# PEER gates marked and gated in one VectorE operation per token, and the last gate tile stored in four portions beside the experts

## The chip, the cores and the metric

The kernel runs on one core of a Trainium2 chip. The metric is the device time of one execution in microseconds (us); lower is better. A core has five engines that run their own instruction streams and meet through semaphores: TensorE (PE, matmuls), VectorE (DVE), ScalarE (ACT), GpSimd (POOL) and SyncE (SP, which here only starts transfers). Sixteen DMA engines move data between HBM (the memory outside) and SBUF (the memory inside, 128 partitions). PSUM is where matmuls leave their results.

## What is computed

The program is a two-part network. Its first part has two layers, each with a mixer and a PEER feed-forward block (a block with 128 x 128 = 16384 tiny experts, of which every token picks 128). Only PEER matters here:

```
def peer_ffn(h, w_query, sub_keys, expert_u, expert_v):
    ...
    idx = jnp.take_along_axis(cand_i, pos, axis=-1).reshape(t_count, PEER_HEADS * PEER_TOPK)
    gate = jax.nn.softmax(top_s, axis=-1).reshape(t_count, PEER_HEADS * PEER_TOPK).astype(h.dtype)
    def block(args):
        tb, ib, gb = args
        act = jax.nn.gelu(jnp.einsum('pkd,pd->pk', expert_u[ib], tb), approximate=False) * gb
        return jnp.einsum('pk,pkd->pd', act, expert_v[ib])
```

A chosen expert's number is first key x 128 + second key. Layer 0 works on 512 tokens, layer 1 on 256.

## The kernel before

**No gather.** The kernel computes all 16384 experts for all tokens, 128 at a time (one first key, called a row here), and multiplies by a gate that is zero where a token did not pick the expert. So it needs the gates spread out: for each first key i, a table [second key, token].

**`peer_scatter`** makes that table. `selT` holds, on 128 partitions (a token's 128 picks), the first key, the second key and the gate of each token. For one token the product of a [pick, second key] matrix B (one-hot of the second key times the gate) and a [pick, first key] matrix A (one-hot of the first key) is its 128 x 128 table of gates. The work goes in sets of 8 tokens with two buffers (x = 0, 1). In one set

- VectorE compares key numbers (bf16) with the second keys (L1752), with the first keys (L1754), and multiplies the second marks by the gates into fp32 `second_ind` (L1758), each for 8 tokens at once, 1024 elements wide;
- ScalarE widens the first marks to fp32 `first_ind` (L1784) and copies two PSUM banks of four tokens each into the stage (L1788);
- TensorE does eight matmuls (L1773; a profile shows each as two records of 128x128).

Sixteen sets are one tile of 128 tokens; layer 0 has four tiles (64 sets), layer 1 two (32 sets), 96 sets in all. A finished tile of 8 MB (64 KB in each partition) is stored by SP to the HBM tensor `gates` [first key, second key, token] (L1816) in pieces of 512 B, out of two stages in turn. Only the last store of a layer has nothing of `peer_scatter` beside it: SP waits for it (L1818) before the block ends. After its last tile ScalarE and VectorE also split the normed activations into two terms (`TwoTerms`, L1841 to L1851).

**`experts_wide`** (layer 0) and **`experts_narrow`** (layer 1) then run over the 128 rows. SP loads row i's weights `u_stream` and `v_stream` (512 KB each) and its gates `g_stream` (256 KB wide, 128 KB narrow: contiguous 2 KB or 1 KB in each partition). ScalarE and VectorE split u into two parts (L1967 and L2015 wide, L2172 and L2212 narrow), TensorE forms dots (L1929, L2133), ScalarE applies Gelu, VectorE the gate (L2026, L2218), both split that too and v (L1973, L2020; L2184, L2223), and TensorE multiplies with v (L1942, L2143). Wide, the dots of row groups of four are formed ahead; narrow, of two rows ahead. Nothing of these loads starts before `peer_scatter` has ended. Buffers of the experts lie in SBUF where the stages were.

Order on each engine is the order written; a `Fori` is a loop on the chip.

Of the kernel before, what the change touches and what calls it, by code (L numbers as in the profile page):

```python
# [48 lines left out]
class Signal:  # L49
# [9 lines left out]
    def done(self, n):  # L59
        self.base += n  # L60
# [474 lines left out]
class AdaParams:  # L535
# [9 lines left out]
    def __init__(self, k, ctx, layer, ada_w, params, consts, mod, fetch=True, first=0, groups=6 * D // BANK):  # L545
# [5 lines left out]
        self.slot = [k.sig(f"ada_slot{n}") for n in range(self.TURN)]  # L551
# [1153 lines left out]
def peer_scatter(k, selT, T, consts, gates, even, terms):  # L1705
# [8 lines left out]
    GROUP = 2 * SET  # L1714
    TURNS = P // GROUP
    ALL = tiles * TURNS
    first, widened, second, gated, joined, taken = (
        k.sig("sc_" + x) for x in ("first", "widened", "second", "gated", "joined", "taken"))
    ready = k.sig("sc_keys")
    written = [k.sig("sc_written0"), k.sig("sc_written1")]  # L1720
    with ExitStack() as ctx:
        stage = (even, k.sb(ctx, "gate_stage_odd", [P, P]))
        numbers = k.sb(ctx, "key_numbers", [P, 2], BF16)
        keys = k.sb(ctx, "keys_16", [2, T], BF16)
        is_first = k.sb(ctx, "is_first", [2, SET // 2, P, 2], BF16)
        is_second = k.sb(ctx, "is_second", [2, SET // 2, P, 2], BF16)
# [4 lines left out]
        number4 = numbers[:].rearrange("p (q n) a -> p q n a", q=1).broadcast_to([P, SET // 2, P, 2])  # L1731

        def here(i, x):
            return bass.ds(i * GROUP + SET * x, SET)

        def by_token(marks):
            return marks.rearrange("p q n a -> p q a n")

        with nc.Block() as block:
            @block.vector  # L1740
            def _(dve):
                dve.sem_inc(gated.h, 2)
                dve.tensor_copy(numbers[:], C("iota").rearrange("p (n a) -> p n a", a=1).broadcast_to([P, P, 2]))
                dve.tensor_copy(keys[:], selT[:, 0:2, :]).then_inc(ready.h, 1)
                dve.wait_ge(ready.h, ready.at(1))
                with dve.Fori(0, ALL) as i:
                    for x in range(2):
                        def marks(row):
                            return keys[:, row, here(i, x)].rearrange("p (q n a) -> p q n a", n=1, a=2).broadcast_to([P, SET // 2, P, 2])

                        dve.wait_ge(gated.h, gated.at(1 + x) + i * 2)
                        dve.tensor_tensor(is_second[:, x], number4, marks(1), ALU.is_equal).then_inc(second.h, 1)  # L1752
                        dve.wait_ge(widened.h, widened.at(1 + x) + i * 2)
                        dve.tensor_tensor(is_first[:, x], number4, marks(0), ALU.is_equal).then_inc(first.h, 1)  # L1754
                        dve.wait_ge(second.h, second.at(1 + x) + i * 2)
                        dve.wait_ge(joined.h, joined.at(2 * x + 2) + i * 4)
                        gate = selT[:, 2, here(i, x)].rearrange("p (q a n) -> p q a n", n=1, a=2).broadcast_to([P, SET // 2, 2, P])
                        dve.tensor_tensor(B[:, x].rearrange("p (q a) n -> p q a n", a=2), by_token(is_second[:, x]), gate, ALU.mult).then_inc(gated.h, 1)  # L1758
                terms.vector(dve)

            @block.tensor
            def _(pe):
                pe.sem_inc(joined.h, 4)
                with pe.Fori(0, ALL) as i:
                    for b in range(4):
                        x = b // 2
                        if b % 2 == 0:
                            pe.wait_ge(widened.h, widened.at(3 + x) + i * 2)
                            pe.wait_ge(gated.h, gated.at(3 + x) + i * 2)
                        pe.wait_ge(taken.h, taken.at(1 + b) + i * 4)  # L1770
                        for a in range(4):
                            n = 4 * (b % 2) + a
                            m = pe.matmul(ps[:, b, a * P:a * P + P], B[:, x, n], A[:, x, n], start=True, stop=True)  # L1773
                        m.then_inc(joined.h, 1)

            @block.scalar
            def _(act):
                act.sem_inc(taken.h, 4)
                act.sem_inc(widened.h, 2)

                def widen(i, x):
                    act.wait_ge(first.h, first.at(1 + x) + i * 2)
                    act.wait_ge(joined.h, joined.at(2 * x + 2) + i * 4)
                    act.activation(A[:, x].rearrange("p (q a) n -> p q a n", a=2), by_token(is_first[:, x]), ACT.Copy).then_inc(widened.h, 1)  # L1784

                def take(i, tile, at, b):
                    act.wait_ge(joined.h, joined.at(5 + b) + i * 4)
                    act.activation(stage[tile % 2][:, :, bass.ds(at + 4 * b, 4)], ps[:, b, :].rearrange("p (t n) -> p n t", t=4), ACT.Copy).then_inc(taken.h, 1)  # L1788

                for tile in range(tiles):  # L1790
                    t0 = tile * TURNS
                    widen(t0, 0)
                    widen(t0, 1)
                    if tile >= 2:
                        act.wait_ge(written[tile % 2].h, written[tile % 2].at(DMA_DONE * (tile // 2)))
                    take(t0, tile, 0, 0)
                    take(t0, tile, 0, 1)
                    with act.Fori(0, TURNS - 1) as n:
                        i = n + t0
                        at = n * GROUP  # L1800
                        widen(i + 1, 0)
                        take(i, tile, at, 2)
                        take(i, tile, at, 3)
                        widen(i + 1, 1)
                        take(i + 1, tile, at + GROUP, 0)
                        take(i + 1, tile, at + GROUP, 1)
                    take(t0 + TURNS - 1, tile, P - GROUP, 2)
                    take(t0 + TURNS - 1, tile, P - GROUP, 3)
                act.wait_ge(written[0].h, written[0].at(DMA_DONE * (tiles // 2)))
                terms.scalar(act)  # L1810

            @block.sync
            def _(sp):
                for tile in range(tiles):
                    sp.wait_ge(taken.h, taken.at(4 + (tile + 1) * TURNS * 4))
                    sp.dma_start(gates[:, :, tile * P:tile * P + P].rearrange("i p t -> p i t"), stage[tile % 2][:]).then_inc(written[tile % 2].h, DMA_DONE)  # L1816
                for w in written:
                    sp.wait_ge(w.h, w.at(DMA_DONE * tiles // 2))  # L1818
    terms.done()
    ready.done(1)  # L1820
    for x in (first, second):
        x.done(2 * ALL)
    for x in (gated, widened):
        x.done(2 * ALL + 2)
    for x in (joined, taken):
        x.done(4 * ALL + 4)
    for w in written:
        w.done(DMA_DONE * tiles // 2)
# [29 lines left out]
def experts_wide(k, u, v, gates, h, acc, xT, gain, us):  # L1858
# [10 lines left out]
    with ExitStack() as ctx:  # L1869
        ub = k.sb(ctx, "u_stream", [4, DC, P])  # L1870
        vb = k.sb(ctx, "v_stream", [2, D])
        vs = k.sb(ctx, "v_parts", [4, 2, D], F32R)
        gb = k.sb(ctx, "g_stream", [4, T])
        act = k.sb(ctx, "acts", [2, T])
# [3 lines left out]
        with nc.Block() as block:  # L1878
            @block.sync
            def _(sp):  # L1880
# [5 lines left out]
                def get_g(s, j, first):  # L1886
                    if not first:
                        sp.wait_ge(gated.h, s * 4 + gated.at(j - 3))
                    sp.dma_start(gb[:, j], gates[bass.ds(s * 4 + j, 1)].rearrange("a p t -> (a p) t")).then_inc(g_in[j].h, DMA_DONE)
# [72 lines left out]
            def _(sc):  # L1962
# [120 lines left out]
def experts_narrow(k, u, v, gates, h, xT, gain, us, spare, ident):  # L2083
# [12 lines left out]
    with ExitStack() as ctx:  # L2096
        ub = k.sb(ctx, "u_stream", [RAW, DC, P])
        vb = k.sb(ctx, "v_stream", [RAW, D])
        vs = k.sb(ctx, "v_parts", [RING, 2, D], F32R)
        act = k.sb(ctx, "acts", [RING, T])  # L2100
        aparts, gb = spare
        sums = vb[:, 0:2]
        pd = k.banks(ctx, 4, "pd")
        po = k.banks(ctx, 4, "po")
        with nc.Block() as block:
            @block.sync
            def _(sp):
                def get(n, j, first):
                    if not first:
                        sp.wait_ge(u_split.h, n + u_split.at(j + 1 - RAW))  # L2110
                    sp.dma_start(ub[:, j], u[bass.ds(n + j, 1)].rearrange("a p c e -> p (a c) e")).then_inc(u_in[j].h, DMA_DONE)
                    if not first:
                        sp.wait_ge(gated.h, n + gated.at(j + 1 - RAW))
                    sp.dma_start(gb[:, j], gates[bass.ds(n + j, 1)].rearrange("a p t -> (a p) t")).then_inc(g_in[j].h, DMA_DONE)
                    if not first:
# [1166 lines left out]
```

## Time and profile before

| what | value |
|---|---|
| runs before | 4536.93, 4542.0, 4542.59 us (median 4542.0) |
| span of the profiled execution | 4538.3 us, between the fastest and the median of these runs |
| PE, DVE, ACT busy | 3652.0 (80%), 2230.0 (49%), 1566.0 (35%) us |
| DMA | 909.64 MB in 331813 packets, mean 200 GB/s |
| scatter, layer 0 | from about 996 us to the last tile's store at 1151.54 us |
| scatter, layer 1 | to the last tile's store at 2588.33 us |
| one store of 8192 KB | 30.3 us from issue to landing |

The profile times the instructions of one execution. Its span runs from the first to the last of them; the page gives no other time of that execution, so the span stands beside the runs of the kernel as it is. PE's share is an average over stages with different limits; what counts for this change is what is waited for in the two scatters and just behind them.

### The profile page before, as it was taken

To read this page: it belongs to the slowest core of one execution; us is meant where nothing else is said; L and a number is where in the kernel's file an instruction comes from. 1 tells how busy PE (TensorE), PEld (TensorE's weight loads), DVE (VectorE), ACT (ScalarE), POOL (GpSimd) and SP (SyncE) were. 2 spreads that over 40 slices of the span, in tenths; PEclk is the share of its full clock that TensorE was granted. 3 is DMA by queue.
4 is the path that set the end of the run, shared out by engine and by line. 5 is a ranking of instruction groups with operands and counts; after the bars stand their busy time and mean duration, and the time that the engine had idled before them with its cause. 6 is when DMAs were issued, how large, how long until landed. Compare 5 with 4: busy or idle time off the path is not lost. (4 is left out here: it accounts for less than half of the span.)

```text
span 4538.3 us, 58330 instructions
## 1 busy us (share of the span) xinstructions
PE 3652.0 (80%) x19637; PEld 2640.8 (58%) x19637; DVE 2230.0 (49%) x4378; ACT 1566.0 (35%) x2639; POOL 168.9 (4%) x344
## 2 busy tenths in 40 slices
PE   5977977968699999998796689998368667777776
PEld 3747965447588888886565579997236322222223
DVE  3634643899566666665358778884441100000001
ACT  3433432128444444443241666663121111011111
POOL 0006610000000000000000000000000000000000
PEclk8988988979899999999897899999659788788878
DMA  4230021516644454443201499994212499999996
GB/s 161 73 132 13 13 96 52 210 45 199 217 175 182 185 185 175 168 173 126 98 20 65 126 362 312 312 312 140 116 38 84 189 428 427 427 427 428 427 428 273
DMA packets 331813, 909.64 MB, mean 200 GB/s; under 512 B 46592, under 2 KB 167168, under 8 KB 306176
## 3 DMA queue, kind: packets, MB, share of 16 engines
q1 hardware_dynamic: 331648, 907.42, 52.9%
q8 instruction: 106, 1.74, 0.2%
q14 instruction: 59, 0.48, 0.0%
HBM read 854.38 MB, written 52.95 MB: 200 GB/s over the span
## 5 line engine op out<-in xcount | busy, mean ns | idle before, releaser
L1929 PE MATMUL pd<-h_parts,u_parts 128*128 128x512 f32 x2048 | 471.3, 390 | 37.5 <-DVE u_parts L2015 37.5
L1942 PE MATMUL po<-act_parts,v_parts 128*128 128x512 f32 x2048 | 483.6, 393 | 10.3 <-DVE v_parts L2020 3.7
L1929 PEld LDWEIGHTS pd<-h_parts,u_parts 128*128 128x128 f32 x2048 | 385.6, 188 | 118.1 <-DVE u_parts L2015 37.7
L1942 PEld LDWEIGHTS po<-act_parts,v_parts 128*128 128x128 f32 x2048 | 383.6, 189 | 105.4 <-DVE v_parts L2020 22.4
L3053 PE MATMUL pb<-moe_ring,moe_xs 128*32 128x512 f32 x2048 | 334.4, 759 | 137.1 <-DMA moe_ring<-in_moe_gu 119.3
L3104 DVE TENSOR_TENSOR moe_hidden<-moe_silu,pg 128x512 f32<-128x512 f32 x16 | 11.0, 688 | 659.6 <-PE pg L3042 533.1
L2133 PE MATMUL pd<-h_parts,u_parts 128*128 128x256 f32 x2048 | 268.2, 284 | 38.6 <-DVE u_parts L2212 38.6
L2133 PEld LDWEIGHTS pd<-h_parts,u_parts 128*128 128x128 f32 x2048 | 264.6, 192 | 50.3 <-DVE u_parts L2212 39.2
L2143 PE MATMUL po<-v_parts,act_parts 128*128 128x512 f32 x1024 | 260.0, 398 | 0.9 <-DVE act_parts L2228 0.9
L395 PE MATMUL ps<-h_terms,w_terms 128*128 128x512 f32 x960 | 225.1, 398 | 40.6 <-DVE w_terms L408 40.6
L3069 PE MATMUL pd<-moe_ring,moe_hidden 128*32 128x512 f32 x1024 | 167.4, 790 | 100.6 <-DMA moe_ring<-in_moe_down 87.9
L1979 ACT ACTIVATE acts<-pd 128x512 f32<-128x512 f32 x128 | 76.7, 599 | 486.0 <-PE pd L1929 486.0
L395 PEld LDWEIGHTS ps<-h_terms,w_terms 128*128 128x128 f32 x960 | 184.8, 193 | 81.5 <-DVE w_terms L408 42.5
L3089 ACT ACTIVATE moe_part<-pb 128x512 f32<-128x512 f32 x128 | 76.3, 597 | 451.4 <-PE pb L3053 451.3
L3053 PEld LDWEIGHTS pb<-moe_ring,moe_xs 128*32 128x32 f32 x2048 | 67.0, 124 | 280.7 <-DMA moe_ring<-in_moe_gu 142.6
L1773 PE MATMUL ps<-first_ind,second_ind 128*128 128x128 f32 x1536 | 198.2, 284 | 38.9 <-ACT first_ind L1784 28.9
L3042 PEld LDWEIGHTS pg<-consts,moe_part 128*128 128x128 f32 x1024 | 140.5, 215 | 130.9 <-issue 129.6
L1773 PEld LDWEIGHTS ps<-first_ind,second_ind 128*128 128x128 f32 x1536 | 182.2, 195 | 55.3 <-issue 54.9
L2143 PEld LDWEIGHTS po<-v_parts,act_parts 128*128 128x128 f32 x1024 | 185.3, 190 | 35.2 <-DVE v_parts L2223 1.1
L2040 DVE TENSOR_TENSOR hT<-hT,po 128x512 f32<-128x512 f32 x248 | 159.1, 682 | 90.1 <-PE po L1942 90.0
L1538 PE MATMUL pq<-hT,w_stream 128*128 128x512 f32 (+1 forms) x512 | 173.3, 498 | 27.0 <-PEq L568 15.0
L2223 DVE SCALAR_TENSOR_TENSOR v_parts<-v_stream,v_parts 128x1024 fp32r<-128x1024 f32 x128 | 156.8, 1225 | 63.4 <-ACT v_parts L2184 63.4
(472 smaller groups left out, 5846.8 us busy)
## 6 DMA issues: line engine op xcount, KB each, us to landing
moe_ring<-in_moe_gu SPq DMA_DIRECT2D x128, 2048.0 KB, 26.3
u_stream<-in_peer_u SPq DMA_DIRECT2D x256, 512.0 KB, 6.0
v_stream<-in_peer_v SPq DMA_DIRECT2D x256, 512.0 KB, 4.3
moe_ring<-in_moe_down SPq DMA_DIRECT2D x64, 2048.0 KB, 26.2
ada_ring<-in_ada_w SPq DMA_DIRECT2D x24, 2048.0 KB, 13.4
g_stream<-peer_gates SPq DMA_DIRECT2D x128, 256.0 KB, 5.9
peer_gates<-gate_stage_even SPq DMA_DIRECT2D x3, 8192.0 KB, 30.3
peer_gates<-gate_stage_odd SPq DMA_DIRECT2D x3, 8192.0 KB, 30.3
```

The lines of the kernel that those rows point to most:

```text
L395: m = pe.matmul(ps[:, ch % BANKS, 0:T], ws[:, r, w, c], parts[:, x, c], start=(c + w + x == 0), stop=(c == kc - 1 and w == 1))
L1538: m = pe.matmul(pq[:, ch % 2, 0:T], stream.wb[:, g % 2, c, (ch % 4) * P:(ch % 4) * P + P], hT[:, c, 0:T], start=(c == 0), stop=(c == DC - 1))
L1773: m = pe.matmul(ps[:, b, a * P:a * P + P], B[:, x, n], A[:, x, n], start=True, stop=True)
L1929: m = pe.matmul(pd[:, j, 0:T], us[:, j, w, c], h[:, w, c], start=(c + w == 0), stop=(c == DC - 1 and w == 1))
L1942: m = pe.matmul(po[:, (c + b) % 4, 0:T], vs[:, j, w, (c + b) * P:(c + b) * P + P], aparts[:, 4 * half + j, w], start=(j + w == 0), stop=(j ...
L2040: dve.tensor_tensor(acc[:, c], acc[:, c], po[:, c % 4, 0:T], ALU.add).then_inc(added.h, 1)
L2133: m = pe.matmul(pd[:, j % RING, 0:T], us[:, j % RING, w, c], h[:, w, c], start=(c + w == 0), stop=(c == DC - 1 and w == 1))
L2143: m = pe.matmul(po[:, 2 * t + half], aparts[:, r, w, t * P:t * P + P], vs[:, r, w, half * BANK:half * BANK + BANK], start=(start and w == ...
L2223: dve.scalar_tensor_tensor(out=vs[:, j % RING, 1], in0=vb[:, j], scalar=FAR / STEP, in1=vs[:, j % RING, 0].bitcast(F32), op0=ALU.mult, op1 ...
L3042: m = pe.matmul(pg[:, n // 4, a * CAP:a * CAP + CAP], part[:, n % 2, j * P:j * P + P], stacked, start=True, stop=True)
L3053: m = pe.matmul(pb[32 * q:32 * q + 32, n % 2, :], xs[:, u % 2, c], w[:, c, :], start=(c < 4), stop=(c >= 4))
L3069: m = pe.matmul(pd[32 * j:32 * j + 32, b, :], hid[:, a * CAP:a * CAP + CAP], w[:, j, b * BANK:(b + 1) * BANK], start=(g == 0), stop=(g == ...
```

## The change

It has four parts.

1. **VectorE in a set.** The comparison of second keys and the multiplication with gates for 8 tokens become eight `tensor_scalar` operations, one a token: fp32 key numbers 0 to 127 compared with a [128, 1] operand (the second key of each partition) and multiplied with another (the gate). Bf16 first marks are made for 6 of 8 tokens only and widened by ScalarE as before, now 768 elements; for the other two tokens VectorE writes `first_ind` itself with a `tensor_scalar` that has one [128, 1] operand. The loops are written out.
2. **Layout of `gates`.** Now [tile, second key, first key, token in tile]: a stage goes out as 64 KB contiguous in each partition, and a row's gates come in as pieces of 512 B, one per partition and tile.
3. **The last tile.** ScalarE starts its store itself in four portions (first keys 0 to 31, 32 to 63, ...), each with its own semaphore, ahead of its share of `TwoTerms`, and the block does not wait for them. The experts wait portion by portion where they read gates or overwrite the stage.
4. **Places in SBUF** of the experts' buffers are ordered for that, and the narrow ones are halved.

```
-                with dve.Fori(0, ALL) as i:
-                    for x in range(2):
-                        ...
-                        dve.tensor_tensor(is_second[:, x], number4, marks(1), ALU.is_equal).then_inc(second.h, 1)
-                        dve.tensor_tensor(is_first[:, x], number4, marks(0), ALU.is_equal).then_inc(first.h, 1)
-                        dve.tensor_tensor(B[:, x].rearrange("p (q a) n -> p q a n", a=2), by_token(is_second[:, x]), gate, ALU.mult).then_inc(gated.h, 1)
+                for n in range(ALL):
+                    x, t0 = n % 2, n * SET
+                    marks = keys[:, t0:t0 + WIDE].rearrange("p (q n a) -> p q n a", n=1, a=2).broadcast_to([P, PAIRS, P, 2])
+                    if n >= 2:
+                        dve.wait_ge(widened.h, widened.at(n - 1))
+                    dve.tensor_tensor(is_first[:, x], number4, marks, ALU.is_equal).then_inc(first.h, 1)
+                    if n >= 2:
+                        dve.wait_ge(joined.h, joined.at(2 * n - 2))
+                    for j in range(SET):
+                        if j >= WIDE:
+                            dve.tensor_scalar(A[:, x, j], iota, key(0, t0 + j), None, ALU.is_equal)
+                        m = dve.tensor_scalar(B[:, x, j], iota, key(1, t0 + j), key(2, t0 + j), ALU.is_equal, ALU.mult)
+                        if j % 4 == 3:
+                            m.then_inc(gated.h, 1)
...
+                act.wait_ge(taken.h, taken.at(2 * ALL))
+                last.write(act, gates, stage[(tiles - 1) % 2])
                 act.wait_ge(written[0].h, written[0].at(DMA_DONE * (tiles // 2)))
                 terms.scalar(act)
...
-                    sp.dma_start(gates[:, :, tile * P:tile * P + P].rearrange("i p t -> p i t"), stage[tile % 2][:]).then_inc(written[tile % 2].h, DMA_DONE)
+                    sp.dma_start(gates[tile], stage[tile % 2][:]).then_inc(written[tile % 2].h, DMA_DONE)
...
+    def write(self, eng, gates, stage):
+        for n in range(self.PARTS):
+            rows = slice(n * self.ROWS, (n + 1) * self.ROWS)
+            eng.dma_start(gates[self.tile, :, rows], stage[:, rows]).then_inc(self.landed[n].h, DMA_DONE)
...
 # experts_wide, SP
                 for j in range(4):
+                    get_u(1, j, False)
+                last.wait(sp, 0)
+                for j in range(4):
                     get_g(0, j, True)
-                for j in range(4):
-                    get_u(1, j, False)
                 period(0, True)
+                last.wait(sp, 1, 2, 3)
...
 # experts_wide, ScalarE
                     high_u(1, j)
+                    if j == 0:
+                        last.wait(sc, 1, 2, 3)
                     high_a(0, 0, j, True)
...
 # experts_narrow, SP
+                for j in range(HALF):
+                    get_u(0, j)
+                last.wait(sp, 0)
+                for j in range(HALF):
+                    get_g(0, j)
+                    get_v(0, j)
+                for j in range(HALF, RAW):
+                    get_g(0, j)
+                last.wait(sp, 1, 2)
+                for j in range(HALF, RAW):
+                    get_u(0, j)
+                last.wait(sp, 3)
+                for j in range(HALF, RAW):
+                    get_v(0, j)
```

HALF is 4 and RAW 8. In `experts_narrow` ScalarE waits for portion 1 before it splits v of row 2.

VectorE, at the beginning of the scatter of layer 0, before: one turn of the loop, two sets (ISA and REGISTER_ALU rows are waits and their arithmetic).

```order
L1752 TENSOR_TENSOR is_second<-key_numbers,keys_115 128x1024
L1754 ISA
L1754 TENSOR_TENSOR is_first<-key_numbers,keys_115 128x1024
L1756 ISA
L1758 ISA
L1758 TENSOR_TENSOR second_ind<-is_second,sel_T 128x1024
```

And of the change, the same place, one set:

```order
L1747 TENSOR_TENSOR is_first<-key_numbers,keys_116 128x768
L1753 TENSOR_SCALAR second_ind<-consts,sel_T 128x128 x6
L1752 TENSOR_SCALAR first_ind<-consts,sel_T 128x128
L1753 TENSOR_SCALAR second_ind<-consts,sel_T 128x128
L1752 TENSOR_SCALAR first_ind<-consts,sel_T 128x128
L1753 TENSOR_SCALAR second_ind<-consts,sel_T 128x128
```

Three operations of a set have become eleven, ten of them 128 elements wide.

SyncE, at the end of the scatter of layer 0 and the start of `experts_wide`, before:

```order
L1816 DMA peer_gates<-gate_stage_even 128x128x128
L1816 DMA peer_gates<-gate_stage_odd 128x128x128
L1739 UNCONDITIONAL_BRANCH
L1879 UNCONDITIONAL_BRANCH
L1884 DMA u_stream<-in_peer_u 128x1024 x4
L1889 DMA g_stream<-peer_gates 128x512 x4
L1884 DMA u_stream<-in_peer_u 128x1024 x4
```

And of the change:

```order
L1805 DMA peer_gates<-gate_stage_odd 128x16384
L1805 DMA peer_gates<-gate_stage_even 128x16384
L1733 UNCONDITIONAL_BRANCH
L1890 UNCONDITIONAL_BRANCH
L1895 DMA u_stream<-in_peer_u 128x1024 x8
L1900 DMA g_stream<-peer_gates 128x4x128 x4
```

The fourth store has left SP's queue, all eight first u loads stand ahead of the gates, and a gate load is 128 x 4 pieces.

ScalarE, at the end of the scatter of layer 1, of the change:

```order
L1831 DMA peer_gates<-gate_stage_odd 128x4096 x4
L1862 ACTIVATE h_parts<-hT 128x256 x8
L1733 UNCONDITIONAL_BRANCH
L2209 UNCONDITIONAL_BRANCH
L2216 ACTIVATE u_parts<-u_stream 128x1024 x3
L2222 ACT_TABLE_LOAD
```

The four portions stand ahead of the eight ACTIVATEs of `TwoTerms`; before, those followed the last copy directly.

## Rows read from the trace of the kernel before

**Rows 1.** Windows: a scatter tile, wide experts, start and middle of narrow experts.

```profile
1037.00:1075.00 38.00, 32.54 (x259) 29.79 (x257) 37.65 (x49) 32.61 (x49) 0.00 (x0) 1.00 0.76 221
1500.00:1800.00 300.00, 298.67 (x1304) 243.68 (x1303) 198.54 (x243) 126.28 (x163) 0.00 (x0) 1.00 0.48 175
2640.00:2700.00 60.00, 60.00 (x383) 54.46 (x382) 51.56 (x67) 42.46 (x66) 0.00 (x0) 1.00 1.04 397
2900.00:3000.00 100.00, 100.00 (x635) 90.57 (x634) 82.39 (x106) 68.18 (x106) 0.00 (x0) 1.00 0.90 309
```

Columns: stretch, length, busy us (and instructions) of PE, PEld, DVE, ACT, POOL, granted TensorE clock, DMA share, GB/s.

**Rows 2.** Timeline of one scatter set of layer 0 (start us, us, instruction, count).

```profile
1141.45 0.68 DVE L1752 TENSOR_TENSOR is_second<-key_numbers,keys 128x1024 bf16<-128x1024 bf16 x1
1141.49 1.06 ACT L1788 ACTIVATE gate_stage_odd<-ps 128x512 f32 x2
...
1141.77 2.05 PE L1773 MATMUL ps<-first_ind,second_ind 128*128 128x128 f32 x16 [0.29 <-ACT first_ind L1784]
1142.06 0.68 DVE L1754 TENSOR_TENSOR is_first<-key_numbers,keys 128x1024 bf16<-128x1024 bf16 x1
1142.66 1.22 DVE L1758 TENSOR_TENSOR second_ind<-is_second,sel_T 128x1024 f32<-128x1024 bf16 x1
1142.85 1.06 ACT L1784 ACTIVATE first_ind<-is_first 128x1024 f32<-128x1024 bf16 x1 [0.30 <-DVE is_first L1754]
1143.80 0.68 DVE L1752 TENSOR_TENSOR is_second<-key_numbers,keys 128x1024 bf16<-128x1024 bf16 x1
```

**Rows 3.** Groups by line and shape, VectorE (busy us, mean ns; idle before).

```profile
L1758 DVE TENSOR_TENSOR second_ind<-is_second,sel_T 128x1024 f32<-128x1024 bf16 x96 | 116.7, 1215 | 2.6 <-PE ps L1773 2.6
L2419 DVE TENSOR_SCALAR att_s<-att_s,att_stats 128x512 f32<-128x512 f32 x32 | 15.6, 486 | 1.1
L2419 DVE TENSOR_SCALAR att_s<-att_s,att_stats 128x256 f32<-128x256 f32 x24 | 8.5, 353 | 0.9
L1841 DVE TENSOR_SCALAR hT<-hT 128x256 f32<-128x256 f32 x8 | 1.7, 280 | 0.0
```

**Rows 4.** Timeline, two trains of eight VectorE operations.

```profile
2382.37 3.26 DVE L526 SCALAR_TENSOR_TENSOR hT<-xT,mod_mult,rstd 128x256 f32<-128x256 f32 x8
2585.31 1.69 DVE L1841 TENSOR_SCALAR hT<-hT 128x256 f32<-128x256 f32 x8
```

**Rows 5.** Timeline from the last store of layer 0 to the first dots.

```profile
1151.41 4.26 ACT L1851 ACTIVATE h_parts<-hT 128x512 fp32r<-128x512 f32 x8
1151.54 0.37 SPq L1816 DMA_DIRECT2D peer_gates<-gate_stage_odd  x1
1152.06 4.90 DVE L1845 SCALAR_TENSOR_TENSOR h_parts<-h_parts,hT 128x512 fp32r<-128x512 f32 x8 [0.74 <-ACT h_parts L1851]
1182.35 1.77 SPq L1884 DMA_DIRECT2D u_stream<-in_peer_u  x4
...
1185.97 1.06 ACT L1967 ACTIVATE u_parts<-u_stream 128x1024 fp32r<-128x1024 f32 x1 [30.31 <-DMA u_stream<-in_peer_u]
...
1188.34 26.82 PE L1929 MATMUL pd<-h_parts,u_parts 128*128 128x512 f32 x110 [37.47 <-DVE u_parts L2015]
```

**Rows 6.** The same in layer 1, and the dots of row 4.

```profile
2588.20 2.55 ACT L1851 ACTIVATE h_parts<-hT 128x256 fp32r<-128x256 f32 x8
2588.33 0.38 SPq L1816 DMA_DIRECT2D peer_gates<-gate_stage_odd  x1
2588.64 2.77 DVE L1845 SCALAR_TENSOR_TENSOR h_parts<-h_parts,hT 128x256 fp32r<-128x256 f32 x8 [1.55 <-ACT h_parts L1851]
2619.13 0.35 SPq L2111 DMA_DIRECT2D u_stream<-in_peer_u  x1
...
2625.22 3.74 PE L2133 MATMUL pd<-h_parts,u_parts 128*128 128x256 f32 x16 [37.55 <-DVE u_parts L2212]
...
2640.93 2.08 PE L2133 MATMUL pd<-h_parts,u_parts 128*128 128x256 f32 x16
```

**Rows 7.** DMA in 4100 to 4400 us, where packets of 16 KB are loaded.

```profile
DMA packets 8800, 128.26 MB, mean 428 GB/s; under 512 B 972, under 2 KB 972, under 8 KB 972
```

More of the change, by code:

```diff
@@ L1713, in peer_scatter @@
     SET = 8
[L1714 to L1718, printed above, removed]
+    PAIRS = 3
+    WIDE = 2 * PAIRS
+    PER = P // SET
+    ALL = tiles * PER
+    first, widened, gated, joined, taken = (k.sig("sc_" + x) for x in ("first", "widened", "gated", "joined", "taken"))
     ready = k.sig("sc_keys")
@@ L1729, in peer_scatter @@
         ps = k.banks(ctx, 4)
[L1731 to L1737, printed above, removed]
+        number4 = numbers[:].rearrange("p (q n) a -> p q n a", q=1).broadcast_to([P, PAIRS, P, 2])
+        iota = C("iota")
         with nc.Block() as block:
@@ L1790, in _, with widen @@
[L1790 to L1794, printed above, removed]
-                        act.wait_ge(written[tile % 2].h, written[tile % 2].at(DMA_DONE * (tile // 2)))
[L1796 to L1808, printed above, removed]
+                def widen(n):
+                    act.wait_ge(first.h, first.at(n + 1))
+                    if n >= 2:
+                        act.wait_ge(joined.h, joined.at(2 * n - 2))
+                    act.activation(A[:, n % 2, 0:WIDE].rearrange("p (q a) n -> p q a n", a=2),
+                                   is_first[:, n % 2].rearrange("p q n a -> p q a n"), ACT.Copy).then_inc(widened.h, 1)
@@ new lines, in take @@
+                def take(n, b):
+                    tile, at = n // PER, (n % PER) * SET + 4 * b
+                    act.wait_ge(joined.h, joined.at(2 * n + b + 1))
+                    act.activation(stage[tile % 2][:, :, at:at + 4], ps[:, 2 * (n % 2) + b, :].rearrange("p (t n) -> p n t", t=4), ACT.Copy).then_inc(taken.h, 1)
+                widen(0)
+                widen(1)
+                for n in range(ALL):
+                    tile = n // PER
+                    if n % PER == 0 and tile >= 2:
+                        act.wait_ge(written[tile % 2].h, written[tile % 2].at(DMA_DONE * (tile // 2)))
+                    take(n, 0)
+                    take(n, 1)
+                    if n + 2 < ALL:
+                        widen(n + 2)
@@ L1855, in done, with experts_wide @@
         self.high.done(DC)
-def experts_wide(k, u, v, gates, h, acc, xT, gain, us):
+def experts_wide(k, u, v, gates, h, acc, xT, gain, us, last):
     nc = k.nc
@@ L2080, in experts_wide, with experts_narrow @@
     added.done(N_SUPER * DC)
-def experts_narrow(k, u, v, gates, h, xT, gain, us, spare, ident):
+def experts_narrow(k, u, v, gates, h, xT, gain, us, spare, ident, last):
     nc = k.nc
@@ L2107, in _ @@
             def _(sp):
[L2108 to L2115, printed above, removed]
-                        sp.wait_ge(v_split.h, n + v_split.at(j + 1 - RAW))
-                    sp.dma_start(vb[:, j], v[bass.ds(n + j, 1)].rearrange("a p d -> (a p) d")).then_inc(v_in[j].h, DMA_DONE)
@@ L2188, in high_a, with step @@
                     sc.activation(aparts[:, j % RING, 0], act[:, j % RING], ACT.Copy, scale=1.0 / FAR).then_inc(a_high.h, 1)
-                def step(n, j, start=False, last=False):
+                def step(n, j, start=False, end=False):
                     early = start and j < RING
-                    if not (last and j >= TURN - 2):
+                    if not (end and j >= TURN - 2):
                         high_u(n, j + 2, start and j + 2 < RING)
                     squash(n, j, early)
+                    if start and j == 2:
+                        last.wait(sc, 1)
                     high_v(n, j, early)
```

158 lines of the change are left out of this document (88 added, 70 removed).

## The prediction

> **What bounds the kernel now.** I read the windows first. In a scatter tile VectorE is busy 37.65 of 38.00 us, TensorE 32.54 and ScalarE 32.61; the clock is full and the DMA engines have room [rows 1]. The timeline of one set then shows who waits: VectorE's operations touch each other and the set repeats after 1143.80 - 1141.45 = 2.35 us, while ScalarE waits 0.30 us for VectorE's first marks and TensorE 0.29 us for ScalarE [rows 2]. So VectorE's three steps, 0.61 + 0.60 + 1.14 us from start to start, are the scatter, in 96 sets [rows 2, 3]. Behind it comes a hole: the last store is issued at 1151.54, the first u load at 1182.35 and the first dots are formed at 1188.34; in layer 1 it is 2588.33, 2619.13 and 2625.22 [rows 5, 6]. TensorE stands still for 37.5 us each time, 30.8 of it the store. Behind that TensorE is full (298.67 of 300 us wide, 100 of 100 narrow), with DMA at 0.48 and 0.90 of its time [rows 1]. The change touches both places, VectorE's work and the hole, and loads gates in smaller pieces where TensorE is full.
>
> **Part 1: a set on VectorE.** What counts is the time from start to start. No row shows a 128-element `tensor_scalar` with [128, 1] operands in a train, so I build it up. Without such an operand, 256 wide: (1.69 - 0.28)/7 = 0.201 us [rows 3, 4]. From 512 to 256 elements the same operation loses 486 - 353 = 133 ns, so 128 fewer are worth 67 ns, and a 128-wide one takes 0.134 us; of that 0.067 us is fixed [rows 3]. A [128, 1] operand: eight 256-wide operations with one take 3.26 us, eight without 2.77 us, that is 0.061 us each [rows 4, 6]; the durations 353 and 280 ns say 0.073 [rows 3]. So 0.195 us with one operand. The bf16 comparison shrinks to 768 elements: (0.61 - 0.07) x 0.75 + 0.07 = 0.475 us. A set is then 0.475 + 10 x 0.195 = 2.425 us if a second operand costs nothing more, against 2.34: +0.085 x 96 = **+8 us**. This is the term that decides, and its bounds are wide:
>
> - Below, the operand costs nothing in such a train: 0.475 + 10 x 0.134 = 1.82 us. Then others bound the set. ScalarE needs 2.35 - 0.30 = 2.05 us now, and its widening loses 256 elements at (4.26 - 2.55)/8 = 0.214 us per 256 [rows 5, 6]: 1.83. TensorE's 16 records take 2.05 us with the tail, about 1.9 in a train [rows 2]. With hand-overs some 1.95 us: -0.39 x 96 = -37 us.
> - Above, the second operand costs another 0.061 us: 0.475 + 8 x 0.256 + 2 x 0.195 = 2.91 us, +0.57 x 96 = +55 us.
>
> I take the middle, since both rows with one operand show its price and none shows it hidden, and two operands side by side may well be fetched in one go. The Trainium skill speaks to both sides. "VectorE: DVE Perf Modes" (section on the TRN2 errata) gives 58 + elements/2 cycles at 0.96 GHz for such an operation, operands or not, 0.127 us; by it a set would be 1.75 us on VectorE, which is the lower bound's case; the 0.061 us in this trace is not in that formula. "ScalarE: Activation LUTs" (what ACT_TABLE_LOAD costs) says that on ScalarE each [128, 1] operand adds its own time; carried over to VectorE that would be the upper bound's case. No row here shows two.
>
> The ends of the scatter get shorter. Now, after VectorE's last 1.22 us operation eight matmuls and a copy follow; then only four do, and the first matmul of a layer waits for four small operations instead of two comparisons and a wide product. I estimate 2 us a layer, **-4 us**. Written-out loops cost only fetching of instructions; nothing shows a wait for that now, zero.
>
> **Parts 2 and 3: the store.** It moves 8.39 MB. With 512 B pieces it takes 30.3 us (277 GB/s). With pieces of 16 KB the load stretch reaches 428 GB/s [rows 7], which would be 19.6 us; no row shows such a store, so its bounds are 19.6 and 30.3; I take 20, as the piece size is that of the 428 row.
>
> *Layer 0.* Count from the last copy. ScalarE issues four portions, as SP's four u loads do in 1.77 us [rows 5]; so `TwoTerms`, hidden until now, ends not 5.4 but 7.2 us after it (1152.06 + 4.90 = 1156.96 before). This is the price of losing its cover. SP issues u at 7.7; the first dots could be formed 6.0 us later, at 14. But the store shares the DMA engines. Before the dots of row 4 can be formed, store, five u rows (2.6 MB) and four gate rows (1.05 MB) are to be moved, 12.1 MB, 28 us at 428 GB/s: at 30 + 2.4 for the split = 32. Before, they were formed at 36.8 + 2 for the low clock + 4 x 3.68 = 53.5 (a row's dots are half of 300/1304 x 32 = 7.36 us [rows 1]). Gain 21. ScalarE's wait for portions 1 to 3 behind row 0 holds the split of u for row 5 and every gate product behind it; with the store landed by 25 it costs little, I take 18. With a store at 277 GB/s the same sum gives 38.9 + 2 + 2.4, gain 10.
>
> *Layer 1.* Before u of row 4 is there: the store, u and v of four rows (4.2 MB), eight gate rows (1.05) and u (0.5), 14.2 MB, 33 us, so dots of row 4 at 37 against 2640.93 - 2588.33 = 52.6 [rows 6]: gain 15. With the slow store 47, gain 6. Together **-33 us**, bounds -16 and -48 (dots at 14 and 11.5 us instead of 36.8 and 36.9, if nothing of the store stood in the way).
>
> *Gate loads in 512 B pieces.* Narrow, a row needs 1.18 MB in 3.78 us. When pressed, the DMA engines moved 397 GB/s [rows 1], 2.97 us a row. If 128 KB of gates go at the old store's 277 GB/s they need 0.47 us, at 428 0.31: at most 0.2 more. Room is 0.8 us, cost nothing. Wide has twice the room. If that cover were gone, each 0.1 us over 3.78 would cost 13 us.
>
> **Sum.** +8 - 4 - 33 = -29 us against the profile's span of 4538.3, which lies 3.7 under the median; against the median 4542 this gives 4513.
>
> **Rivals.**
>
> - *The operand is hidden*: a set of 1.95 us, -37 instead of +8: 4538 - 37 - 4 - 33, against the median 4468. For it: the eight operations depend on nothing near. Against: the 0.061 us in a train of independent ones.
> - *The second operand costs as much as the first*: +55 - 4 - 33 = +18, 4560. It is slower from 2.73 us a set on, that is from 0.04 us for the second operand. This is the one on the other side. For it: nothing shows two at once. Against: nothing either.
> - *The store stands in the way of the experts' first loads.* Four portions are queued first and may be served first; then the hole is filled hardly at all and the gain of 33 shrinks to some 10: +8 - 4 - 10, 4536. For it: no row shows a store beside loads. Against: the pressed windows show three kinds of loads from one queue sharing 397 GB/s [rows 1], and pieces of 16 KB leave more of that than pieces of 512 B.
> - *Gathered gates are slow.* Pieces of one partition pair lie 64 KB apart. Above 1.3 us for 128 KB (under 100 GB/s) narrow rows wait for DMA; at 80 GB/s 1.64 us, +0.3 x 128 = +40: 4553. "DMA: Bandwidth & Descriptors" (Latency and other measured facts) in the Trainium skill reports copies that slow to 207 GB/s and less where rows lie 512 KB and more apart. The old store wrote pieces 256 KB apart and reached 277 GB/s.
>
> **How the numbers follow.** Forecast 0.45 (4513, its own range 4500 to 4528), operand hidden 0.27, second operand paid 0.14, store in the way 0.09, slow gathers 0.05. The range 4462 to 4545 holds the first, second and fourth, 0.81. A measurement of this kernel tells about 0.2%, 9 us, from no change. Faster by more: 0.45 + 0.27 + 0.04 (half of the fourth) = 0.76 and a little; same: 0.06; slower: 0.17, the second operand and most of the slow gathers.
>
> **What would show it.** The scatter tile's length in the windows: 38.8 us if right, 31 if the operand is free, 46 if paid twice. A 128-wide `tensor_scalar` with two operands should last 0.28 us and repeat after 0.195. TensorE's idle before the first dots should fall from 37.5 us to some 16 in both layers, followed by short waits in rows 1 to 5. Portions should land in about 5 us each. Narrow rows must keep 3.78 us; if they don't, the gathers are slow. I am wrong above all if the pitch of the two-operand operation is not near 0.195 us.

## The result and the profile after

The changed kernel is slower: 4568.09 us (median of 4 runs, 4566.57 to 4572.35) against 4541.89 for the kernel before (4 runs beside it, 4536.93 to 4542.59), ratio 1.0062, 95% interval 1.0048 to 1.0075. The forecast of 4513 has the wrong sign, and its range ended at 4545. The profiled execution took 4566.57 us with a span of 4564.7, 26.4 more than the span of 4538.3 before.

Windows of the changed kernel: a scatter tile, narrow experts, and the second network from the update of x at the end of layer 1 to the first matmuls of its own experts (columns as in [rows 1]).

```profile
1040.00:1085.00 45.00, 35.25 (x248) 29.81 (x248) 45.00 (x172) 28.49 (x48) 0.00 (x0) 1.00 0.44 187
2700.00:3000.00 300.00, 300.00 (x1920) 273.36 (x1920) 249.58 (x321) 206.44 (x321) 0.00 (x0) 1.00 0.94 322
3137.60:3603.50 465.90, 292.04 (x1118) 209.21 (x1122) 161.42 (x409) 85.08 (x221) 0.73 (x2) 0.72 0.21 78
```

VectorE is now busy 45.00 of 45.00 us, and TensorE and ScalarE for a smaller share than before. The timeline of one set (start us, us, instruction; in brackets how long the engine stood idle before it, and what ended that):

```profile
1080.24 0.55 DVE L1747 TENSOR_TENSOR is_first<-key_numbers,keys 128x768 bf16<-128x768 bf16 x1
...
1080.71 1.62 DVE L1753 TENSOR_SCALAR second_ind<-consts,sel_T 128x128 f32<-128x128 f32 x6
1080.83 0.84 ACT L1778 ACTIVATE first_ind<-is_first 128x768 f32<-128x768 bf16 x1 [1.09 <-DVE is_first L1747]
...
1081.92 1.13 PE L1769 MATMUL ps<-first_ind,second_ind 128*128 128x128 f32 x8 [0.38 <-ACT first_ind L1778]
1082.25 0.28 DVE L1752 TENSOR_SCALAR first_ind<-consts,sel_T 128x128 f32<-128x128 f32 x1
1082.44 0.34 DVE L1753 TENSOR_SCALAR second_ind<-consts,sel_T 128x128 f32<-128x128 f32 x1
1082.70 0.28 DVE L1752 TENSOR_SCALAR first_ind<-consts,sel_T 128x128 f32<-128x128 f32 x1
1082.89 0.34 DVE L1753 TENSOR_SCALAR second_ind<-consts,sel_T 128x128 f32<-128x128 f32 x1
1083.15 0.55 DVE L1747 TENSOR_TENSOR is_first<-key_numbers,keys 128x768 bf16<-128x768 bf16 x1
```

The set repeats after 1083.15 - 1080.24 = 2.91 us, to the hundredth the upper bound of the forecast, against 2.34 of before; a tile of sixteen sets takes 46.6 us. An operation with one operand lasts 0.28 us, with two 0.34. From start to start the comparison takes 0.47, one with one operand 0.19 to 0.20, and one with two (1.62 - 0.34)/5 = 0.256.

The end of layer 0's scatter and the first dots, where [rows 5] stood:

```profile
1183.51 0.60 ACT L1784 ACTIVATE gate_stage_odd<-ps 128x512 f32<-128x512 f32 x1 [0.80 <-PE ps L1769]
1184.14 3.17 ACTq L1831 DMA_DIRECT2D peer_gates<-gate_stage_odd  x4
...
1187.40 4.27 ACT L1862 ACTIVATE h_parts<-hT 128x512 fp32r<-128x512 f32 x8 [3.30 <-issue]
1188.07 4.91 DVE L1856 SCALAR_TENSOR_TENSOR h_parts<-h_parts,hT 128x512 fp32r<-128x512 f32 x8 [3.04 <-ACT h_parts L1862]
1193.23 21.92 SPq L1895 DMA_DIRECT2D u_stream<-in_peer_u  x8
1205.69 1.06 ACT L1980 ACTIVATE u_parts<-u_stream 128x1024 fp32r<-128x1024 f32 x1 [14.02 <-DMA u_stream<-in_peer_u]
...
1208.06 30.87 PE L1942 MATMUL pd<-h_parts,u_parts 128*128 128x512 f32 x128 [24.59 <-DVE u_parts L2030]
```

TensorE's idle time fell from 37.47 to 24.59 us, and its 128 matmuls of dots (eight rows) then run in one piece. In layer 1, where [rows 6] stood:

```profile
2643.92 3.79 PE L2177 MATMUL pd<-h_parts,u_parts 128*128 128x256 f32 x16 [20.90 <-DVE u_parts L2258]
2650.89 5.58 PE L2177 MATMUL pd<-h_parts,u_parts 128*128 128x256 f32 x32 [3.18 <-DVE u_parts L2258]
...
2664.02 2.64 PE L2177 MATMUL pd<-h_parts,u_parts 128*128 128x256 f32 x16 [1.91 <-DVE u_parts L2258]
```

There the dots begin 20.90 us after the scatter's last matmul (37.55 before), but wait 3.18 us behind row 0 and 1.91 before row 4.

From issue to landing (least, median, most), a full store of the changed kernel and then its eight portions:

```profile
DMA to landing us min/median/max: 22.6/22.7/22.9
```

```profile
DMA to landing us min/median/max: 6.3/14.3/23.4
```

**Where the 26.4 us are.** The traces are cut at the same instructions: the start of VectorE's first operation for the scatter, the end of the last copy out of PSUM, the start of the last addition to the layer's output (layer 0) or of the update of x (layer 1), and the first matmul of the second network's experts. Times are in us.

| stage | before | after | difference |
|---|---|---|---|
| scatter, layer 0 | 156.0 | 189.0 | +33.0 |
| last copy to the last addition, layer 0 | 992.4 | 979.4 | -13.0 |
| scatter, layer 1 | 80.0 | 95.7 | +15.7 |
| last copy to the update of x, layer 1 | 528.5 | 513.7 | -14.8 |
| second network up to its experts | 460.0 | 465.9 | +5.9 |

Scatter +48.7, experts -27.8, second network +5.9: +26.8. The changed kernel reaches its first scatter 0.4 us earlier, and the stretches between the layers and behind the table are the same to 0.1 us.

### The profile page after: what moved, and what is told of

Same layout as the page of the kernel before. It is cut to its first block and busy times, and to the rows that moved or that the text cites. A ratio compares the mean times of both kernels' runs of the same rounds, so it can differ in the third digit from the quotient of the medians.

```text
span 4564.7 us, 57706 instructions
## 1 busy us (share of the span) xinstructions
PE 3671.7 (80%) x19637; PEld 2655.1 (58%) x19637; DVE 2286.7 (50%) x5146; ACT 1545.7 (34%) x2639; POOL 168.0 (4%) x344
## 3 DMA queue, kind: packets, MB, share of 16 engines
q8 instruction: 119, 1.95, 0.2%
## 5 line engine op out<-in xcount | busy, mean ns | idle before, releaser
L1955 PE MATMUL po<-act_parts,v_parts 128*128 128x512 f32 x2048 | 483.4, 393 | 10.5 <-DVE v_parts L2035 3.9
L1942 PE MATMUL pd<-h_parts,u_parts 128*128 128x512 f32 x2048 | 471.3, 390 | 24.6 <-DVE u_parts L2030 24.6
L1769 PE MATMUL ps<-first_ind,second_ind 128*128 128x128 f32 x1536 | 222.4, 290 | 63.1 <-ACT first_ind L1778 34.6
L1753 DVE TENSOR_SCALAR second_ind<-consts,sel_T 128x128 f32<-128x128 f32 x768 | 221.9, 343 | 0.0
```

Of the source, the lines that this page charges most:

```text
L1753: m = dve.tensor_scalar(B[:, x, j], iota, key(1, t0 + j), key(2, t0 + j), ALU.is_equal, ALU.mult)
L1769: m = pe.matmul(ps[:, 2 * x + b, a * P:a * P + P], B[:, x, 4 * b + a], A[:, x, 4 * b + a], start=True, stop=True)
L1942: m = pe.matmul(pd[:, j, 0:T], us[:, j, w, c], h[:, w, c], start=(c + w == 0), stop=(c == DC - 1 and w == 1))
L1955: m = pe.matmul(po[:, (c + b) % 4, 0:T], vs[:, j, w, (c + b) * P:(c + b) * P + P], aparts[:, 4 * half + j, w], start=(j + w == 0), stop=(j ...
```

## The experiments

My theory after the result: VectorE sets the scatter, and every [128, 1] operand of a `tensor_scalar` costs 0.06 us for itself, the second as much as the first. A rival is that the second ALU operation of the instruction costs the time; another, that something else holds the sets. The kernel before ran again, 13 times beside the first four kernels (median 4539.58) and 13 times beside the last four (4538.69). Intervals are of 95%; where a row of a stage is named, it is as in the table above.

### The gate's operand left out

```
-  m = dve.tensor_scalar(B[:, x, j], iota, key(1, t0 + j), key(2, t0 + j), ALU.is_equal, ALU.mult)
+  m = dve.tensor_scalar(B[:, x, j], iota, key(1, t0 + j), 1.0, ALU.is_equal, ALU.mult)
```

> The change, but the eight operations of a set multiply with the immediate 1.0 instead of the gate operand: gates are left out, marks alone are spread. Theory 1 (the price hangs on the number of [128, 1] operands): start to start 0.195 instead of 0.255 us, a set of 2.43 us, 46 us less than the change, 4522 us. Rival (the price hangs on the second ALU operation): 0.255 us stays and so does 4568 us.

Measured: 4521.0 us (4517.2 to 4523.91), ratio to before 0.9956, interval 0.9939 to 0.9973. It leaves the gates out; the work of the engines is otherwise the same. The timeline of VectorE:

```profile
1081.21 0.54 DVE L1747 TENSOR_TENSOR is_first<-key_numbers,keys 128x768 bf16<-128x768 bf16 x1
1081.68 1.25 DVE L1753 TENSOR_SCALAR second_ind<-consts,sel_T 128x128 f32<-128x128 f32 x6
...
1083.64 0.55 DVE L1747 TENSOR_TENSOR is_first<-key_numbers,keys 128x768 bf16<-128x768 bf16 x1
```

The set is 2.43 us, and the operation repeats after (1.25 - 0.27)/5 = 0.196 us. The multiplication is still in it, by 1.0, so the 0.06 us hang on the operand and not on the second ALU operation. The set is, to 0.01 us, the one I had forecast for the real kernel.

### Both operands left out

```
-  m = dve.tensor_scalar(B[:, x, j], iota, key(1, t0 + j), key(2, t0 + j), ALU.is_equal, ALU.mult)
+  m = dve.tensor_scalar(B[:, x, j], iota, float(j), 1.0, ALU.is_equal, ALU.mult)
```

> As the run without gates, and the key is an immediate too, so the eight operations have no [128, 1] operand (second keys and gates are left out). Theory 1: start to start 0.134 us; VectorE needs 0.475 + 0.39 + 8 x 0.134 = 1.94 us, close to TensorE's 1.9 and ScalarE's 1.83, a set of about 2.0 us, 87 us less than the change, 4481 us. Rival (a floor for 128-wide operations near 0.19 us whatever their operands): the same as without gates, 4522 us.

Measured: 4473.96 us in one run, span 4472.1. VectorE's timeline:

```profile
1079.46 0.56 DVE L1747 TENSOR_TENSOR is_first<-key_numbers,keys 128x768 bf16<-128x768 bf16 x1
1079.94 0.91 DVE L1753 TENSOR_SCALAR second_ind<-consts 128x128 f32<-128x128 f32 x6
...
1081.41 0.56 DVE L1747 TENSOR_TENSOR is_first<-key_numbers,keys 128x768 bf16<-128x768 bf16 x1
```

(0.91 - 0.23)/5 = 0.136 us, and the set 1.95. The three prices 0.136, 0.196 and 0.256 lie on a line. The sum of VectorE's operations, 0.47 + 8 x 0.136 + 2 x 0.20, is the set, so down to 1.95 us no other engine holds it, and operand by operand the time of the scatter follows.

### All first marks made wide

```
-    PAIRS = 3
+    PAIRS = 4
```

All eight first marks are then made by the bf16 comparison and widened by ScalarE (256 words more are kept free ahead of the odd stage).

> The change, but bf16 marks for all eight first keys, widened by ScalarE; VectorE makes none of them itself. Theory 1: 0.61 + 8 x 0.255 = 2.65 us a set against 2.91, 25 us less, 4543 us. Rival (ScalarE, with 2.05 us of work and its hand-overs, holds the set longer): 2.8 us or more, 4557 us.

Measured: 4541.21 us (10 runs, 4535.97 to 4543.75), ratio 1.0003, interval 0.9993 to 1.0012.

```profile
1079.91 0.69 DVE L1747 TENSOR_TENSOR is_first<-key_numbers,keys 128x1024 bf16<-128x1024 bf16 x1
1080.51 2.14 DVE L1753 TENSOR_SCALAR second_ind<-consts,sel_T 128x128 f32<-128x128 f32 x8
1082.56 0.69 DVE L1747 TENSOR_TENSOR is_first<-key_numbers,keys 128x1024 bf16<-128x1024 bf16 x1
```

The set is 2.65 us. Two operations of 0.196 us for 0.13 us of a wide comparison were a loss of 0.26 us a set, 25 us in 96 sets: of the 49 us that the scatter grew by, about half come from taking two first keys into VectorE. ScalarE had the room for them.

Its second network, with the same code, took 460.9 us against 465.9 of the changed kernel, at a granted clock of 0.74 against 0.72:

```profile
3114.50:3575.50 461.00, 287.25 (x1118) 205.03 (x1122) 161.32 (x409) 85.07 (x221) 0.73 (x2) 0.74 0.21 79
```

### The old marks with the new store

```
+    dve.tensor_tensor(is_second[:, x], number4, marks(1), ALU.is_equal)
     dve.tensor_tensor(is_first[:, x], number4, marks(0), ALU.is_equal)
-    for j in range(SET):
-        ...
+    gate = selT[:, 2, t0:t0 + SET].rearrange(...).broadcast_to([P, PAIRS, 2, P])
+    dve.tensor_tensor(B[:, x].rearrange(...), is_second[:, x].rearrange(...), gate, ALU.mult)
```

Only VectorE's part is undone (PAIRS is 4, 1536 words more are kept free ahead of the odd stage). Stages, portions and loads are those of the change.

> The change, but with VectorE's marks and gates made 8 tokens at a time as in the kernel before (loops written out, all first keys by ScalarE); layout, portions and waits of the change are kept. Theory 1 (the second [128, 1] operand costs another 0.061 us, so a set takes 2.91 us, and that is all that the change lost): sets of 2.34 us, a layer-0 tile of 37.5 us, 0.57 x 96 = 55 us less than the change, 4513 us. Rival (something in the new layout or the portions costs time in the experts): 4530 us or more.

Measured: 4514.43 us (4511.33 to 4521.01), ratio 0.9945, interval 0.9928 to 0.9962. But for kernels that leave work out, it is the fastest here together with the one that issues three portions later (4513.27, below). The scatter takes 154.3 and 79.0 us, 1.7 and 1.0 less than before, and the experts 978.6 and 518.0 against 992.4 and 528.5, -24.3 us. The parts add up: the store's is a gain of 24 to 28 us, VectorE's a loss of 49 to 51. The next four kernels are built on this one, and their timelines are to be held against its own:

```profile
1144.58 0.60 ACT L1787 ACTIVATE gate_stage_odd<-ps 128x512 f32<-128x512 f32 x1 [0.29 <-PE ps L1772]
...
1154.31 20.62 SPq L1898 DMA_DIRECT2D u_stream<-in_peer_u  x7
1166.76 1.06 ACT L1983 ACTIVATE u_parts<-u_stream 128x1024 fp32r<-128x1024 f32 x1 [14.01 <-DMA u_stream<-in_peer_u]
...
1169.13 6.04 PE L1945 MATMUL pd<-h_parts,u_parts 128*128 128x512 f32 x16 [24.59 <-DVE u_parts L2033]
```

Its last copy ends at 1144.58 + 0.60 = 1145.18, and its first dots begin 23.95 us later (20.3 in layer 1).

### All portions waited for before the block ends

```
                 for tile in range(max(0, tiles - 3), tiles - 1):
                     sp.wait_ge(written[tile % 2].h, written[tile % 2].at(DMA_DONE * (tile // 2 + 1)))
+                last.wait(sp, 0, 1, 2, 3)
```

> The kernel with the old VectorE method in the new structure (4514 us), with one wait added: SyncE waits for all four portions before the scatter block ends, so nothing of the experts starts beside the store. Theory 1 (starting the experts beside the store gained 13 us in layer 0 and 15 in layer 1 in the change's trace, against a 30.3 us store): the portions need some 20 us, so the block ends about 20 + 3 us behind the last copy and dots 6 us later, at 30 instead of 24 and 20 us: 4514 + 6 + 10 = 4530 us; the layout (pieces of 64 KB) and not the overlap gave the rest. Rival (the overlap gave all of it): 4542 us.

Measured: 4519.79 us (4515.16 to 4521.43), ratio 0.9957, interval 0.9941 to 0.9974.

```profile
1145.85 3.17 ACTq L1835 DMA_DIRECT2D peer_gates<-gate_stage_odd  x4
...
1167.44 7.81 SPq L1899 DMA_DIRECT2D u_stream<-in_peer_u  x5
...
1174.94 1.65 PE L1946 MATMUL pd<-h_parts,u_parts 128*128 128x512 f32 x3 [29.75 <-DVE u_parts L2034]
```

No load runs beside the store, and still all but 5.4 us of the gain are there (6.3 in the two stretches of experts). With four runs of each, from 4511 to 4521 us, so small a difference is hardly clear of noise. My expectation was too high by 10. The store is over 21.6 us after its first portion's issue, 9 earlier than one with 512 B pieces [rows 5], so the larger pieces (16 KB in a portion) are the bigger half. In layer 1 the dots begin 7.6 us later than with the overlap (27.8 against 20.3 us from the last copy), and x is updated at the same distance (518.1 against 518.0): there the overlap gives nothing that this trace shows, though kernels with the same expert code differ by 4 us in that stretch.

### Portions 1 to 3 behind the split of the activations

ScalarE issues only portion 0 at the end of the scatter, and the other three at the start of the experts:

```
-                last.write(act, gates, stage[(tiles - 1) % 2])
+                last.write(act, gates, stage[(tiles - 1) % 2], (0,))
...
 # experts_wide and experts_narrow, ScalarE
+                last.write(sc, gates, odd, (1, 2, 3))
```

> The kernel with the old VectorE method in the new structure (4514 us), but only portion 0 is issued ahead of TwoTerms; portions 1 to 3 are issued by ScalarE as its first step in the experts, beside SyncE's first u loads. Theory 1 (the first u load took 12.5 us instead of 3.6 because 8 MB were queued ahead of it): first dots some 6 us earlier in both layers, but the portions land 8 us later and ScalarE and SyncE wait for them in rows 1 to 4, so the sum is within 5 us of 4514. Rival (a load is slow beside any store, however late that one is queued): the first dots stay at 24 and 20 us behind the last copy and 4520 us.

Measured: 4513.27 us (4510.34 to 4519.58), ratio 0.9947, interval 0.9931 to 0.9964.

```profile
1145.63 0.60 ACT L1787 ACTIVATE gate_stage_odd<-ps 128x512 f32<-128x512 f32 x1 [0.30 <-PE ps L1772]
...
1152.59 1.90 ACTq L1834 DMA_DIRECT2D peer_gates<-gate_stage_odd  x3
1162.63 1.06 ACT L1983 ACTIVATE u_parts<-u_stream 128x1024 fp32r<-128x1024 f32 x1 [11.62 <-DMA u_stream<-in_peer_u]
...
1165.00 10.37 PE L1945 MATMUL pd<-h_parts,u_parts 128*128 128x512 f32 x32 [19.41 <-DVE u_parts L2034]
1168.72 1.06 ACT L1983 ACTIVATE u_parts<-u_stream 128x1024 fp32r<-128x1024 f32 x1 [5.03 <-DMA u_stream<-in_peer_u]
...
1174.85 1.06 ACT L1983 ACTIVATE u_parts<-u_stream 128x1024 fp32r<-128x1024 f32 x1 [5.08 <-DMA u_stream<-in_peer_u]
```

The last copy ends at 1146.23, so the dots begin 18.8 us behind it in layer 0, and 14.3 in layer 1: 5.2 and 5.9 us earlier than in the kernel it is built on, as expected. In layer 0 that is still 5 us behind the 14 that the forecast had named. The time is the same: ScalarE then waits 5 us each for u of rows 1 and 2, and the experts of layer 0 take 980.6 us against 978.6. Which bytes go first seems only to move the wait about, and what ends last to be the sum of store and first loads.

### Portions issued by SP

```
-                last.write(act, gates, stage[(tiles - 1) % 2])
...
+                sp.wait_ge(taken.h, taken.at(2 * ALL))
+                last.write(sp, gates, stage[(tiles - 1) % 2])
```

> The kernel with the old VectorE method in the new structure (4514 us), but SyncE issues the four portions, so ScalarE's part of TwoTerms follows the last copy at once and the 3.2 us of issuing lie beside it. Theory 1 (the issuing on ScalarE is on the path): up to 3 us less in each layer. Rival (in SyncE's own queue the u loads stand behind all of the store): first dots only 28 to 30 us behind the last copy, 4514 + 10 = 4524 us.

Measured: 4517.55 us (4517.38 to 4520.7), ratio 0.9954, interval 0.9937 to 0.997.

```profile
1151.68 3.05 SPq L1835 DMA_DIRECT2D peer_gates<-gate_stage_odd  x4
1151.69 4.27 ACT L1866 ACTIVATE h_parts<-hT 128x512 fp32r<-128x512 f32 x8
...
1157.52 22.76 SPq L1899 DMA_DIRECT2D u_stream<-in_peer_u  x6
1176.30 1.06 ACT L1984 ACTIVATE u_parts<-u_stream 128x1024 fp32r<-128x1024 f32 x1 [20.34 <-DMA u_stream<-in_peer_u]
```

ScalarE is freed of 3.2 us, and nothing is gained: the first u now stands in one queue with the store and is split 18.8 us after its issue, against 12.5 where ScalarE's queue holds the store (1154.31 to 1166.76 above). Half of the 6.3 us between them is only that u is issued 3.3 us sooner behind the store here; counted from the store's issue, the split comes after 24.6 us against 21.6. The dots begin 27.0 us behind the last copy instead of 23.95 (26.0 instead of 20.3 in layer 1). The store gains by it: no portion lands later than 21.1 us after its issue, against 23.4, and 19.2 where no load ran beside it. The median of 3 us over the kernel it is built on is within the spread of the runs. The Trainium skill ("DMA: Bandwidth & Descriptors", Queues, rings and completion order) says that a DMA engine alternates between the queues that have work and takes what is in one in its order. The sign of the two differences agrees with it; no run here shows how the engines shared their time.

### Half of the products on GpSimd

```
+            @block.gpsimd
+            def _(pool):
+                for n in range(ALL):
+                    ...
+                    pool.tensor_tensor(B[:, x, 4:8].rearrange(...), is_second[:, x, 2:4].rearrange(...), gate, ALU.mult)
```

VectorE multiplies four of the eight tokens, 512 elements, GpSimd the others.

> The kernel with the old VectorE method in the new structure (4514 us), with GpSimd, idle otherwise, multiplying marks with gates for tokens 4 to 7 of each set. Theory 1 (VectorE's 2.34 us are the set): VectorE falls to 0.61 + 0.60 + 0.60 = 1.8 us; ScalarE with 2.05 and TensorE with 1.9 take over; GpSimd's 512 elements take 1.1 to 1.4 us, as in the delta rule's rows. A set of 2.1 us, 23 us less, 4491 us. Rival (GpSimd and VectorE hinder each other, or GpSimd is over 2.3 us): no gain, 4514 us or more.

Measured: 4542.45 us (10 runs, 4536.82 to 4550.64), ratio 1.0009, interval 1.0 to 1.0019; the set is 2.65 us, not the 2.1 expected, and VectorE fills all of it.

```profile
1079.94 1.42 POOL L1771 TENSOR_TENSOR second_ind<-is_second,sel_T 128x512 f32<-128x512 bf16 x1 [1.23 <-DVE is_second L1752]
1080.38 1.52 DVE L1760 TENSOR_TENSOR second_ind<-is_second,sel_T 128x512 f32<-128x512 bf16 x1
...
1081.83 0.68 DVE L1752 TENSOR_TENSOR is_second<-key_numbers,keys 128x1024 bf16<-128x1024 bf16 x1
```

VectorE's 512-element product takes 1.45 us from start to start beside GpSimd's; 1024 elements took 1.14 alone [rows 2]. GpSimd's row ends at 1081.36, and VectorE's next operation starts 0.47 us later; half the old product should need some 0.6 us (an estimate from 1.14 us for 1024 elements). So VectorE seems to have stood for most of the time from 1080.38 until GpSimd was done. The Trainium skill ("SBUF — State Buffer", SBUF: two separate sides) says that such a pair of operations takes a shared port in turn, the later one blocked for the whole of the earlier; the trace agrees roughly. That VectorE stood is an inference from two rows, as spans on POOL are rough; that the two did not run side by side is seen in the 1.45 us.

## Why the prediction was wrong

**The step that failed** is in part 1: "A set is then 0.475 + 10 x 0.195 = 2.425 us if a second operand costs nothing more". It costs as much as the first. Everything else of that line held: the comparison (0.47), one operand (0.195), an operation without any (0.134 forecast, 0.136 measured), and the set of 2.43 us where the gate's operand is left out. The upper bound, 0.475 + 8 x 0.256 + 2 x 0.195 = 2.91, is the measured value. I took the middle although the rows showed a price that had been paid for one operand, twice (0.061 us in a train, 0.073 in the durations), and no row showed one hidden; the argument that two "may well be fetched in one go" had no row at all. On the evidence of the trace the second operand at the first one's price should have been the likeliest case, or as likely. The 0.127 us that the prediction quotes for such an operation, with operands or without, is nearly met without any (0.136) and is half of what two of them make (0.256).

**The rival with that mechanism** gave 4560. It missed by 8, which are three terms:

- *Ends of the scatter*: -4 forecast. The scatter grew by 48.7 us where 0.57 x 96 is 54.7: -6.
- *Store and experts*: -33 forecast, -27.8 measured (bounds -16 and -48). Layer 1 gave -14.8 for -15, but that is in part luck: its dots of row 4 began 40.4 us behind the last copy and not 37, and in the five other kernels with the same experts and the same order of store and loads this stretch gained 10.5 to 11.8. Layer 0 gave -13.0 for -18. Two prices were too small: ScalarE's four issues take 3.17 us and not 1.77, and the first u needs 12.5 us from issue to split beside the store, where alone it was 3.6 [rows 5] to 5.1 (1167.44 to 1172.57 in the kernel that waits for the store). So the dots could not start at 14. The sum of bytes at 428 GB/s would have allowed dots of row 4 at 32; they come at about 24.0 + 2 + 4 x 3.68 = 41, since the late first row is ahead of them. Earlier first dots alone don't bring them forward: in the kernel with three portions behind, the first come at 18.8, and layer 0 gains nothing more (980.6 us against 978.6).
- *The second network*: nothing forecast, +5.9. The change doesn't touch it. The same instructions ran at a granted clock of 0.72 for 0.74 and kept TensorE busy for 292.0 us instead of 286.5, and the kernel with all first marks wide has 460.9 us there. But the other seven kernels have 463.6 to 465.4, so it may be an effect of the change after all, for instance by another moment of the start. This was not tried and stays open; it is 5 us of 26.

**The store in the way** (4536) was half right in its mechanism, a store that delays the first loads, and wrong in its size. Why the gain stayed near the forecast nonetheless is another matter than I had argued: mostly the store itself became shorter, and 18 of 24 us come without any overlap. I had 20 us for it, from a load stretch with 16 KB pieces; four portions in 16 KB pieces took 21.6 with no load beside them, a full tile in 64 KB pieces 22.7, and one in 512 B pieces 30.3.

**Gathered gates** cost nothing, as forecast: narrow, TensorE stays at 300.00 of 300 us at a DMA share of 0.94, and a row (24 matmuls of the 1920) takes 3.75 us. The 1.3 us at which they were to be felt would be 1.1 with the 397 GB/s that the prediction uses beside it; nothing hangs on that. **Written-out loops** show no wait: VectorE has none from one set to the next. **The operand hidden** (4468) is refuted by the 2.91 us; the kernel with no operands at all, at 4474, shows what it would have given.

## What to carry to other kernels

A bound that is itself a measured price for the same kind of thing weighs more than a hope that it is shared: price the second operand like the first until a row says otherwise. Many narrow operations pay their operands once each (here 0.06 us on 0.136), so two 1024-element operations that broadcast the values (0.61 + 1.14 = 1.75 us for eight tokens) beat eight narrow ones that do both steps at once (8 x 0.256 = 2.05); count operands before instructions. And when two streams share the DMA engines, look at what the last byte needs, not at what starts first: larger pieces gave most of the gain of the new store (18 of 24 us), and the order of portions and loads none that was clear of noise.

## What the runs showed of the hardware

- A 128-wide fp32 `tensor_scalar` on VectorE repeats after 0.136, 0.196 or 0.256 us with none, one or two [128, 1] operands; with an immediate in its place the second ALU operation adds nothing.
- An 8 MB store from SBUF takes 30.3 us in 512 B pieces and 22.7 us in 64 KB pieces, each from issue to landing.
- ScalarE needs 3.17 us to issue four portions of 2 MB, and its next ACTIVATE waits for that; SP needs 3.05.
- A load of 512 KB landed within 12.5 us when it was issued 9.1 us behind such a store from another engine's queue, and within 18.8 us when it was issued 5.8 us behind it from the same one: 21.6 and 24.6 us from the store's issue.
- GpSimd's and VectorE's products into fp32, with two SBUF inputs each, did not run side by side: 512 elements on VectorE took 1.45 us beside GpSimd's, where 1024 took 1.14 alone.
